# Gate rows of four gated layers: turned in pieces by VectorE, kept in DRAM and broadcast back, in place of matmuls against the identity

## The chip, the cores and the metric

The kernel runs on one NeuronCore of a Trainium2 chip. The metric is the device time of one execution in microseconds (us), taken as the median of the runs.

## The reference

The program is a chain of two networks over x of 256 rows and 1024 columns, all in float32. The first has four gated layers (pool, neighbourhood attention, convolution, pool), the second has two blocks, each a feed-forward part, a mixer and a second feed-forward part. What the change concerns is the gate of the first network:

```python
for i in range(DEPTH):                       # DEPTH = 4
    shift, scale, gate = _modulation(c, ada_w[i], ada_b[i])      # silu(c) @ w + b, cut in three
    hx = _rmsnorm(x, norm_g[i]) * (1.0 + scale[:, None]) + shift[:, None]
    ...                                      # yx = the layer's mixer of hx
    x = x + gate[:, None] * yx
    if update_ctx:                           # layer 0 alone
        ctx = ctx + cgate * yc
```

So a gate is one vector of 1024 values for each layer (and a second one, for the context rows, in layer 0). It multiplies the columns of the mixer's output, the same for every row.

## The kernel before

**Tiles and weights.** Rows lie on the 128 partitions: tiles t = 0, 1 are x, tiles t = 2, 3 are the context rows, which layers 0 and 1 also project. Each weight matrix comes in groups of 128x1024 float32 (512 KB) through eight slots `raw`. SyncE (SP) sends group g once group g-8 is used up (`send`); ScalarE (ACT) makes `w_hi` from it (`split`, L552), GpSimd (POOL) `w_lo` (`low`, L514), and TensorE (PE) multiplies three times with them (`mm3`, L1140 to L1142). So SP runs eight groups ahead of PE.

**Stages.** The list `PLAN` gives the order: p0_in (16 groups), p0_grp (2), p0_out (8), na_in (32), na_out (8), cv_in (32), cv_out (8), p3_in (16), p3_grp (2), p3_out (8), then the two blocks of the second network. Each engine's program is written out by hand in that order, and the engines meet through semaphores and counts.

**Modulation.** The 24 pieces of the modulation (6 for each layer) are computed beside the projections: `ada_weights(a)` on SP brings 2 MB into four places, two of which are `pt[:, 0:1024]` and `pt[:, 1024:2048]` and one `bias[:, 2048:3072]`; `ada_products` on PE; `ada_block` on VectorE (DVE, L1886 and L1888) puts the result as columns into `mods` (one value on each partition, eight columns each for shift, scale and gate of a layer). The last piece of layers 0 to 3 falls at group 7 of p0_in, group 7 of na_in, group 19 of na_in and group 11 of p3_in (`ADA_AT`).

**From columns to rows.** The sum needs the gate along the free dimension, the same on every partition. `gates` on PE (L1350) multiplies each column, broadcast, with the identity: eight products for a gate, in two PSUM banks, and `gate_rows` on ACT (L691) copies these into `pt`. `gated_sum` on DVE (L2008, L2011) multiplies a PSUM bank of the output projection with `pt` and adds the stream. There are five such calls:

- p0, x rows: between the two pairs of `turn_z(0, ...)`, which turn the product z of the grp stage. In front of the third `turn_z` stands a wait on `acc_free`, which DVE signals when it has made the second half of z (L2083).
- p0, context rows: between the third and the fourth output group of tiles 0 and 1.
- na: between the fourth output group and `last_chunks`, which adds groups 4 to 7 and needs each one's `w_lo`. After its `gate_rows`, ACT issues four loads of `rel_rows` (L557), loads a table (L574), splits three groups and takes the squares for the next layer's norm, on which PE's `turn_tile` waits (L1178).
- cv: behind the last projection block, ahead of the wait on `acc_free` for blocks 6 and 7, the second of which ACT gives after a Silu of two banks (L844).
- p3: as p0 with the x rows alone.

Of the kernel before, what the change touches and what calls it, by code (L numbers as in the profile page):

```python
# [5 lines left out]
F32 = mybir.dt.float32  # L6
# [5 lines left out]
P = 128  # L12
D = 1024
# [148 lines left out]
def program(nc, I, out, marks):  # L162
    na_rows = nc.dram_tensor("na_rows", (GRID_W, NA_ROW), F32, kind="Internal").ap()
    rel_rows = nc.dram_tensor("rel_rows", (LAYERS, P, REL_PITCH), F32, kind="Internal").ap()

    with ExitStack() as ctx:
# [25 lines left out]
        cond = sb("cond", [P, KC, 32])  # L192
        rope = sb("rope", [P, 2, NT, HD])
# [5 lines left out]
        eps = sb("eps", [P, 1])  # L199
        warm = sb("warm", [P, 16])  # L200

# [22 lines left out]
        decay_in = sem("decay_in")  # L224
        out_done = sem("out_done")
# [77 lines left out]
        def gate_bank(key, s, nb):  # L303
            return nb if key[0] == "p" and s == 0 else 4 + nb
# [41 lines left out]
        def _(sp):  # L346
# [31 lines left out]
            def narrow(w, blocks, nw, stage=None, prev=None, order=None):  # L378
# [9 lines left out]
                if stage:  # L388
                    for g in range(4 * blocks):
# [15 lines left out]
                        for a in ada_sent(stage, g):  # L405
                            ada_weights(a)
                    return
# [45 lines left out]

            def pool_weights(j, stage, prev=None):
                narrow(I["pool_w_in"][j], 4, 512, stage, prev)
                grp = I["pool_w_grp"][j].rearrange("g (c p) n -> p g c n", p=P)
                for h in range(2):
                    send(grp[:, 2 * h:2 * h + 2], [[512, 2], [256, 2], [1, 256]])
                wide(I["pool_w_out"][j], 8)

# [5 lines left out]
            for j in range(8):  # L466
# [4 lines left out]
                send(I["na_w_out"][0][j * P:(j + 1) * P, :], [[1, D]])  # L471
            narrow(I["conv_w_in"][0], 8, 512, "cv_in", "na_out", CV_ORDER)
            wide(I["conv_w_out"][0], 8)
            pool_weights(1, "p3_in", "cv_out")
# [66 lines left out]
        def _(act):  # L541
# [144 lines left out]
            def gate_rows(key, s=0):  # L686

                for nb in range(2):
                    act.wait_ge(pe_done, pe_s.count(("gate", key, s, nb)))
                    o = s * 1024 + nb * 512  # L690
                    act.activation(pt[:, o:o + 512], ps[:, gate_bank(key, s, nb), :], ACT.Copy).then_inc(act_done, act_s.one(("gate", key, s, nb)))  # L691

            def pool_layer(name, j, streams):
# [35 lines left out]
                gate_rows(name, 0)  # L729
                high_of_z(0, 2)  # L730
                high_of_z(0, 3)
                if streams > 1:
# [3 lines left out]
                    gate_rows(name, 1)  # L736
# [24 lines left out]
            def na_layer():  # L761
# [53 lines left out]
                gate_rows("na")  # L815

            def conv_layer():
# [28 lines left out]
                gate_rows("cv")  # L846
# [280 lines left out]
        def _(pe):  # L1127
# [222 lines left out]
            def gates(key, l, s=0):  # L1350

                for nb in range(2):
# [1408 lines left out]
```

## Time and profile before

| | |
|---|---|
| median of 3 runs | 1884.04 us (1882.99 to 1884.15) |
| the profiled execution | 1882.47 us, its span 1880.5 us |
| TensorE's mean granted clock | 0.998 |
| busy share of the span: PE, PE weight load, DVE, ACT, POOL | 99%, 82%, 41%, 49%, 72% |
| HBM over the span | 195 GB/s |
| SP's longest total wait | 1322.5 us, for PE to use up a weight group (L1142) |

The span is the time from the first to the last instruction. A busy share counts the time in which an instruction of the engine ran. In a timeline each line gives the start in us, the duration in us (of the whole group, where equal instructions are merged), the engine, the line of the code, the operation, what it writes and reads, and in brackets the idle time before it with what ended it. Matmuls overlap, so the time that one takes from PE is the distance between starts, not its duration. Of an instruction in float32 with 128 columns there are two records for one matmul of the code.

### The profile page before, as it was taken

To read this page: it belongs to the slowest core of one execution; us is meant where nothing else is said; L and a number is where in the kernel's file an instruction comes from. 1 tells how busy PE (TensorE), PEld (TensorE's weight loads), DVE (VectorE), ACT (ScalarE), POOL (GpSimd) and SP (SyncE) were. 2 spreads that over 40 slices of the span, in tenths; PEclk is the share of its full clock that TensorE was granted. 3 is DMA by queue.
4 is the path that set the end of the run, shared out by engine and by line. 5 is a ranking of instruction groups with operands and counts; after the bars stand their busy time and mean duration, and the time that the engine had idled before them with its cause. 6 is when DMAs were issued, how large, how long until landed. Compare 5 with 4: busy or idle time off the path is not lost.

```text
span 1880.5 us, 26918 instructions
## 1 busy us (share of the span) xinstructions
PE 1859.7 (99%) x10442; PEld 1534.1 (82%) x10442; DVE 779.9 (41%) x1421; ACT 916.6 (49%) x1365; POOL 1363.3 (72%) x568
## 2 busy tenths in 40 slices
PE   6999999999999999999999999999999999999999
PEld 5888788888888888888788888888888878888887
DVE  4213522674552440755630432533076563043253
ACT  3224511765455654555554454455355555446442
POOL 2524343456777698979678988879897957898886
PEclk9999999999999999999999999999999999999999
DMA  9762576439748476555455566656755644556663
GB/s 358 256 223 68 188 254 213 121 101 307 258 156 315 141 229 210 191 181 177 151 157 189 158 211 192 194 186 206 222 191 172 192 156 147 188 170 201 191 195 128
DMA packets 194846, 364.07 MB, mean 194 GB/s; under 512 B 32260, under 2 KB 48372, under 8 KB 194164
## 3 DMA queue, kind: packets, MB, share of 16 engines
q1 hardware_dynamic: 191280, 351.72, 58.6%
q10 hardware_dynamic: 3460, 10.88, 1.7%
q8 instruction: 74, 1.21, 0.3%
q14 instruction: 32, 0.26, 0.0%
HBM read 361.50 MB, written 6.10 MB: 195 GB/s over the span
## 4 chain that ended last, share of the span: by engine, by line
PE 96%; DMA 2%; ACT 1%; SPq 1%; DVE 1%; ACTq 0%; issue 0%
PE ps L1140 28%; PE ps L1142 27%; PE ps L1141 27%; PE ps L1158 2%; PE ps L1346 2%; DMA proj<-in_ada_w 1%; PE ps L1811 1%; PE ps L1809 1%; PE ps L1810 1%; PE ps L1725 1%; PE ps L1178 1%; PE ps L1498 1%; PE ps L1469 1%; PE ps L1479 1%; PE ps L1770 1%; SPq L375 1%
## 5 line engine op out<-in xcount | busy, mean ns | idle before, releaser
L514 POOL TENSOR_TENSOR w_lo<-raw,w_hi 128x1024 fp32r<-128x1024 f32 x556 | 1344.3, 2454 | 467.2 <-ACT w_hi L552 466.6
L552 ACT ACTIVATE w_hi<-raw 128x1024 fp32r<-128x1024 f32 x556 | 571.9, 1058 | 420.3 <-DMA raw<-in_ffn_w_up 99.8
L1140 PE MATMUL ps<-w_hi,xt_hi 128*128 128x512 f32 x1888 | 746.4, 395 | 3.3 <-POOL w_lo L514 2.5
L1142 PE MATMUL ps<-w_hi,xt_lo 128*128 128x512 f32 x1888 | 734.0, 389 | 0.0
L1141 PE MATMUL ps<-w_lo,xt_hi 128*128 128x512 f32 x1888 | 733.5, 389 | 0.0
L1140 PEld LDWEIGHTS ps<-w_hi,xt_hi 128*128 128x128 f32 x1888 | 355.3, 188 | 83.9 <-issue 11.2
L1142 PEld LDWEIGHTS ps<-w_hi,xt_lo 128*128 128x128 f32 x1888 | 355.0, 188 | 73.7
L1141 PEld LDWEIGHTS ps<-w_lo,xt_hi 128*128 128x128 f32 x1888 | 355.6, 188 | 68.1
L2307 DVE STREAM_TRANSPOSE ps<-proj 32x256 f32<-32x256 f32 (+1 forms) x384 | 166.6, 434 | 6.5
L1140 PE MATMUL ps<-w_hi,xt_hi_ctx 128*128 128x512 f32 (+1 forms) x432 | 167.6, 388 | 0.2
L1142 PE MATMUL ps<-w_hi,xt_lo_ctx 128*128 128x512 f32 (+1 forms) x432 | 166.7, 386 | 0.0
L1141 PE MATMUL ps<-w_lo,xt_hi_ctx 128*128 128x512 f32 (+1 forms) x432 | 166.7, 386 | 0.0
L2288 DVE TENSOR_TENSOR proj<-proj,ps 128x1024 f32<-128x1024 f32 (+1 forms) x18 | 20.4, 1132 | 252.2 <-PE ps L1142 247.8
L1140 PEld LDWEIGHTS ps<-w_hi,xt_hi_ctx 128*128 128x128 f32 x432 | 81.2, 188 | 17.1 <-DVE xt_lo_ctx L1964 1.0
L1142 PEld LDWEIGHTS ps<-w_hi,xt_lo_ctx 128*128 128x128 f32 x432 | 81.2, 188 | 16.3
L1141 PEld LDWEIGHTS ps<-w_lo,xt_hi_ctx 128*128 128x128 f32 x432 | 81.3, 188 | 15.8
L1886 DVE STREAM_TRANSPOSE qt<-ps 128x128 f32<-128x128 f32 x24 | 7.6, 316 | 148.8 <-PE ps L1158 148.8
L939 ACT ACTIVATE proj<-ps 128x1024 f32<-128x1024 f32 x20 | 20.6, 1028 | 63.9 <-PE ps L1142 63.9
L2021 DVE SCALAR_TENSOR_TENSOR x_res<-ps,x_res 128x512 f32<-128x512 f32 x24 | 16.6, 690 | 79.4 <-PE ps L1142 79.4
L868 ACT ACTIVATE proj<-ps 128x1024 f32 (+1 forms) x15 | 15.4, 1028 | 69.4 <-PE ps L1142 69.4
L2609 DVE TENSOR_TENSOR proj<-proj,ps 128x1024 f32<-128x1024 f32 x12 | 14.7, 1221 | 82.8 <-PE ps L1811 82.8
L521 POOL TENSOR_TENSOR bias<-bias,na_mask 128x1024 f32<-128x1024 f32 x8 | 19.1, 2394 | 32.7 <-DMA bias<-na_rows 32.7
(222 smaller groups left out, 1560.5 us busy)
## 6 DMA issues: line engine op xcount, KB each, us to landing
raw<-in_w_in SPq DMA_DIRECT2D x120, 512.0 KB, 3.6
raw<-in_ffn_w_gate SPq DMA_DIRECT2D x88, 512.0 KB, 4.4
raw<-in_ffn_w_up SPq DMA_DIRECT2D x88, 512.0 KB, 4.3
raw<-in_ffn_w_down SPq DMA_DIRECT2D x88, 512.0 KB, 4.2
pt<-in_ada_w SPq DMA_DIRECT2D x44, 512.0 KB, 5.2
raw<-in_pool_w_in SPq DMA_DIRECT2D x32, 512.0 KB, 8.5
raw<-in_na_w_in SPq DMA_DIRECT2D x32, 512.0 KB, 5.0
raw<-in_conv_w_in SPq DMA_DIRECT2D x32, 512.0 KB, 5.4
```

Of the source, the lines that this page charges most:

```text
L375: sp.dma_start(free(bias[64 * rq:64 * rq + 64, 0:1], [[64, 4], [1, GRID_W]], (hp % 2) * 1024 + h * 512 + t * 256), src).then_inc(bias_in[h ...
L514: pool.tensor_tensor(w_lo[:, s, :], raw[:, s, :], w_hi[:, s, :].bitcast(F32), ALU.subtract).then_inc(lo_done, 1)
L521: pool.tensor_tensor(both, both, free(na_mask[:, 0:1], [[0, 4], [1, SEQ]]), ALU.add).then_inc(bias_masked, 1)
L552: act.activation(w_hi[:, g % SLOTS, :], raw[:, g % SLOTS, :], ACT.Copy).then_inc(hi_done, 1)
L939: act.activation(pj(MIX_ORDER[n] * 512, 512, IN_COLS), pair_of(n), how).then_inc(acc_free[(b + n) % 2], 1)
L1140: pe.matmul(o, h, hi, start=start, stop=False)
L1141: pe.matmul(o, h, lo, start=False, stop=False)
L1142: return pe.matmul(o, c, hi, start=False, stop=stop)
L1158: last = pe.matmul(ps[32 * j:32 * j + 32, bank, 0:P], cond[:, m, :], free(ada_slot(k, a), [[P, 4], [1, 32]], c * 512 + 32 * j), start=m == ...
L1346: last = pe.transpose(ps[:, bank, c * SEQ + t * P:c * SEQ + (t + 1) * P], src(t, c), ident[:])
L2288: return dve.tensor_tensor(h, h, ps[:, at:at + 2, cols_of], ALU.mult)
L2307: last = dve.transpose(to, rows)
```

## The change

`gates` on PE and `gate_rows` on ACT are taken out, all five calls. In their place, for each layer l:

- **DVE** turns 32 columns of `mods` (the scale and gate columns of the layer) in 32x32 blocks into `gate_cols`, one instruction behind the layer's last modulation piece (`gates_turned`), after a wait that this piece has been written; from layer 2 on also a wait that the store of two layers before has ended.
- **SP** stores them with four DMAs, one for each 32 partitions, 16 rows of 128 bytes each (`keep_gates`), to `gate_scratch` in DRAM. It waits for DVE's turning first. It stands: for layer 0 behind the 16 sends of p0_in; for layer 1 in na_in behind the send of group 23; for layer 2 ahead of cv_in; for layer 3 behind the 16 sends of p3_in and ahead of those of p3_grp.
- **SP** brings each gate back with one DMA that reads 4 KB, in pieces of 512 bytes, for every one of 128 partitions (512 KB written; `gate_rows` of SP). It stands behind the eight output weight sends of the layer, after waits for the store and for the modulation weights that used the place. The place is `pt`, for na `bias[:, 2048:3072]`.
- `gated_sum` waits for that DMA in place of ACT's copy.
- `mods` is zeroed at the start, and `eps` moves into the last column of `warm`.

```diff
     na_rows = nc.dram_tensor("na_rows", (GRID_W, NA_ROW), F32, kind="Internal").ap()
+    gate_scratch = nc.dram_tensor("gate_scratch", (DEPTH, KC, 2, P), F32, kind="Internal").ap()
     rel_rows = nc.dram_tensor("rel_rows", (LAYERS, P, REL_PITCH), F32, kind="Internal").ap()
...
         cond = sb("cond", [P, KC, 32])
+        gate_cols = sb("gate_cols", [P, 2, 32])
         rope = sb("rope", [P, 2, NT, HD])
...
         rstat = sb("rstat", [P, 64])
-        eps = sb("eps", [P, 1])
         warm = sb("warm", [P, 16])
+        eps = warm[:, 15:16]
...
         decay_in = sem("decay_in")
+        gate_kept, gate_in = sem("gate_kept"), [sem("gate_in0"), sem("gate_in1")]
         out_done = sem("out_done")
...
-        def gate_bank(key, s, nb):
-            return nb if key[0] == "p" and s == 0 else 4 + nb
+        def gates_kept(l):
+
+            return 16 * 4 * (l + 1)
...
                             ada_weights(a)
+                        if stage == "na_in" and g == 23:
+                            keep_gates(1)
                     return
...
+            def keep_gates(l):
+
+                sp.wait_ge(dve_done, dve_s.count(("gate_cols", l)))
+                for j in range(4):
+                    sp.dma_start(bass.AP(gate_scratch.tensor, 2 * D * l + 32 * j, [[P, 2 * KC], [1, 32]]),
+                                 gate_cols[32 * j + 16:32 * j + 32, l % 2, :]).then_inc(gate_kept, 16)
+
+            def gate_rows(l, slots, free_at):
+
+                sp.wait_ge(gate_kept, gates_kept(l))
+                sp.wait_ge(ada_used, free_at)
+                for s, (where, o) in enumerate(slots):
+                    sp.dma_start(free(where[:, 0:1], [[P, KC], [1, P]], o),
+                                 bass.AP(gate_scratch.tensor, 2 * D * l + P * s, [[0, P], [2 * P, KC], [1, P]])).then_inc(gate_in[s], 16)
+
             def pool_weights(j, stage, prev=None):
                 narrow(I["pool_w_in"][j], 4, 512, stage, prev)
+                keep_gates(3 * j)
                 grp = I["pool_w_grp"][j].rearrange("g (c p) n -> p g c n", p=P)
...
                 wide(I["pool_w_out"][j], 8)
+                gate_rows(3 * j, ((pt, 0), (pt, D))[:2 - j], 4 * max(ADA_AT[stage].values()) + 2)
...
                 send(I["na_w_out"][0][j * P:(j + 1) * P, :], [[1, D]])
+            gate_rows(1, ((bias, 2048),), 4 * max(ADA_AT["na_in"].values()) + 3)
+            keep_gates(2)
             narrow(I["conv_w_in"][0], 8, 512, "cv_in", "na_out", CV_ORDER)
             wide(I["conv_w_out"][0], 8)
+            gate_rows(2, ((pt, 0),), 4 * max(ADA_AT["cv_in"].values()) + 1)
             pool_weights(1, "p3_in", "cv_out")
...
                         "p (c n) -> p c n", c=2), ACT.Copy).then_inc(act_done, act_s.one(("xhi", key, s, k)))
-
-            def gate_rows(key, s=0):
-
-                for nb in range(2):
-                    act.wait_ge(pe_done, pe_s.count(("gate", key, s, nb)))
-                    o = s * 1024 + nb * 512
-                    act.activation(pt[:, o:o + 512], ps[:, gate_bank(key, s, nb), :], ACT.Copy).then_inc(act_done, act_s.one(("gate", key, s, nb)))
...
                 high_of_z(0, 1)
-                gate_rows(name, 0)
                 high_of_z(0, 2)
...
                         high_of_z(1, k)
-                    gate_rows(name, 1)
                     split(3)
...
                 split(1)
-                gate_rows("na")
...
                                        ACT.Silu).then_inc(acc_free[(b + n) % 2], 1)
-                gate_rows("cv")
                 split(1)
...
-            def gates(key, l, s=0):
-
-                for nb in range(2):
-                    bank = gate_bank(key, s, nb)
-                    read_out(bank)
-                    for c in range(4):
-                        col = mods[:, 24 * l + 16 + nb * 4 + c, s:s + 1]
-                        last = pe.matmul(ps[:, bank, c * P:(c + 1) * P], free(col, [[0, P]]), ident[:],
-                                         start=True, stop=True)
-                    last.then_inc(pe_done, pe_s.one(("gate", key, s, nb)))
-                    held[bank] = (act_s, ("gate", key, s, nb))
-
             def pool_layer(name, l, streams):
...
                 turn_z(0, 1)
-                gates(name, l)
                 pe.wait_ge(acc_free[(b + 1) % 2], reads(b + 1))
...
                             turn_z(1, 2 * k + 1)
-                        if k == 2:
-                            gates(name, l, 1)
                 if streams > 1:
...
                 out_group(3)
-                gates("na", 1)
                 last_chunks("na_out", "naz", 4, 8, (0, 1), lambda k: k, "cv")
...
                     block(n)
-                gates("cv", 2)
                 go, bo = G0["cv_out"], B0["cv_out"]
...
             dve.memset(cond[:], 0.0)
+            dve.memset(mods[:], 0.0)
             dve.memset(stat[:], 0.0).then_inc(acc_free[1], 1)
...
+            def gates_turned(l):
+
+                dve.wait_ge(ada_read, ADA_COLS * (l + 1))
+                if l > 1:
+                    dve.wait_ge(gate_kept, gates_kept(l - 2))
+                dve.transpose(gate_cols[:, l % 2, :], free(mods[:, 0:1, 0:1], [[1, 32]], 2 * (24 * l + 8))).then_inc(dve_done, dve_s.one(("gate_cols", l)))
+
             def ada_beside(stage, n):
...
                     ada_block(a, bank_of(B0[stage] + n - 1, 3))
+                    if a % ADA_COLS == ADA_COLS - 1:
+                        gates_turned(a // ADA_COLS)
...
                 if t in (0, 2) and nb == 0:
-                    dve.wait_ge(act_done, act_s.count(("gate", key, t // 2, 1)))
+                    dve.wait_ge(gate_in[t // 2], 16 * (("p0", "na", "cv", "p3").index(key) + 1))
                 v = ps[:, bank_of(B0[stage] + nb, t), :]
-                o = (t // 2) * 1024 + nb * 512
-                dve.tensor_tensor(v, v, pt[:, o:o + 512], ALU.mult).then_inc(dve_done, dve_s.one(("gated", stage, t, nb)))
+                rows, o = (bias, 2048) if key == "na" else (pt, (t // 2) * D)
+                dve.tensor_tensor(v, v, rows[:, o + nb * 512:o + (nb + 1) * 512], ALU.mult).then_inc(dve_done, dve_s.one(("gated", stage, t, nb)))
                 dve.wait_ge(dve_done, dve_s.count(("gated", stage, t, nb)))
```

## Rows read from the trace of the kernel before

**Rows 1.** The page's busy line, and busy time by stretch, 640 us to the end.
```profile
PE 1859.7 (99%) x10442; PEld 1534.1 (82%) x10442; DVE 779.9 (41%) x1421; ACT 916.6 (49%) x1365; POOL 1363.3 (72%) x568
...
640.00:1881.00 1241.00, 1237.37 (x5793) 1020.04 (x5791) 515.92 (x973) 633.37 (x919) 1028.14 (x424) 1.00 0.59 183
```

**Rows 2.** The line of the gate products (L1357) and ACT's copies: count, durations.
```profile
L1357 PE MATMUL ps<-ident,mods x80: 270/276/276, 154.0 to 626.2; 128*128 128x128 f32 x80
...
L691 ACT ACTIVATE pt<-ps x10: 592/597/614, 155.2 to 626.5; 128x512 f32<-128x512 f32 x10
```

**Rows 3.** Timeline of DVE and PE, first gate block of p0.
```profile
153.35 2.36 DVE L2083 TENSOR_TENSOR proj<-ps,proj 128x1024 f32<-128x1024 f32 x2 [3.40 <-PE ps L1142]
...
154.02 1.95 PE L1357 MATMUL ps<-ident,mods 128*128 128x128 f32 x16
155.81 1.04 PE L1346 MATMUL ps<-ident,proj 128*128 128x128 f32 x8
```

**Rows 4.** Timeline of PE, second gate block of p0.
```profile
166.77 1.94 PE L1357 MATMUL ps<-ident,mods 128*128 128x128 f32 x16
168.47 0.48 PE L1140 MATMUL ps<-w_hi,xt_hi 128*128 128x512 f32 x1
```

**Rows 5.** Timeline of PE, POOL and ACT's queue, gate block of na and behind.
```profile
425.53 2.35 POOL L514 TENSOR_TENSOR w_lo<-raw,w_hi 128x1024 fp32r<-128x1024 f32 x1 [2.48 <-ACT w_hi L552]
...
425.56 1.95 PE L1357 MATMUL ps<-ident,mods 128*128 128x128 f32 x16
...
427.56 2.50 ACTq L557 DMA_DIRECT2D rel_rows<-in_rel  x4
...
429.43 0.39 PE L1140 MATMUL ps<-w_hi,xt_hi 128*128 128x512 f32 x1
...
437.42 1.09 PE L1178 MATMUL ps<-ident,proj 128*128 128x128 f32 x8 [0.35 <-ACT proj L602]
```

**Rows 6.** Timeline of PE, ACT and DVE, gate block of cv, first gated sum.
```profile
539.40 1.95 PE L1357 MATMUL ps<-ident,mods 128*128 128x128 f32 x16
...
539.60 1.02 ACT L844 ACTIVATE proj<-ps 128x1024 f32<-128x1024 f32 x1 [1.85 <-PE ps L1142]
...
541.11 0.48 PE L1140 MATMUL ps<-w_hi,xt_hi_ctx 128*128 128x512 f32 x1
...
556.01 0.70 DVE L2008 TENSOR_TENSOR ps<-ps,pt 128x512 f32<-128x512 f32 x1 [5.97 <-issue]
```

**Rows 7.** Timeline of DVE and PE, gate block of p3.
```profile
623.86 1.22 DVE L2083 TENSOR_TENSOR proj<-ps,proj 128x1024 f32<-128x1024 f32 x1 [1.65 <-PE ps L1142]
...
624.53 1.95 PE L1357 MATMUL ps<-ident,mods 128*128 128x128 f32 x16
...
626.32 1.04 PE L1346 MATMUL ps<-ident,proj 128*128 128x128 f32 x8
```

**Rows 8.** Timelines in p3: SP's send, DVE's last modulation piece, ACT's splits, ACT's Silu.
```profile
593.25 0.37 SPq L356 DMA_DIRECT2D raw<-in_pool_w_grp  x1
...
600.95 0.61 DVE L1888 TENSOR_TENSOR mods<-qt,cols 128x4 f32<-128x4 f32 x1
...
604.44 3.89 ACT L552 ACTIVATE w_hi<-raw 128x1024 fp32r<-128x1024 f32 x4
...
614.40 1.02 ACT L710 ACTIVATE proj<-ps 128x1024 f32<-128x1024 f32 x1 [6.07 <-PE ps L1142]
```

**Rows 9.** DMA: landing of two p3_grp sends, two small issues, a 4 KB row broadcast.
```profile
DMA to landing us min/median/max: 5.7/6.3/7.0
...
652.85 1.24 SPq L430 DMA_DIRECT2D mix_cols<-in_b_k_norm  x2
...
qt<-in_final_g ACTq DMA_DIRECT2D x1, 512.0 KB, 10.0
```

**Rows 10.** PE busy by stretch: start:end, length, busy (count), granted clock, DMA.
```profile
14.10:16.40 2.30, 1.17 (x36) 1.00 1.03 386
...
17.80:22.00 4.20, 3.72 (x40) 0.59 1.02 371
```

## The prediction, made before the changed kernel ran

> **What bounds the kernel now.** I read the page's busy line first: TensorE is busy for 99% of the span, the next engine for 72% [rows 1]. The chain that ended last runs almost wholly through PE. So time is won only where PE's own queue gets shorter, and lost only where PE begins to wait. From 640 us on PE is busy 1237.4 of 1241.0 us [rows 1] and the change touches nothing there, so what is won ahead of 640 us should reach the end whole. The second view is the line of the gate products: 80 records, which is 5 blocks of 16 [rows 2]. The third are the timelines around each block, where I look for the thing that would hold PE next if the block were gone. That is the whole question here.
>
> **What a block costs.** Between two groups of transposes the 16 records take 155.81 - 154.02 = 1.79 us of PE [rows 3], and the same in p3, 626.32 - 624.53 [rows 7]. Between matmuls with split weights it is 168.47 - 166.77 = 1.70 us [rows 4], and the first matmul behind the block starts its successor a little late, so I take 1.79 for all. Five blocks are 8.95 us, the most that the removal can give. ACT's ten copies of 0.6 us [rows 2] leave too. ACT is half idle, so they count only where ACT stands in front of PE.
>
> **Block by block.** A wait answered by another engine costs PE about 0.06 us; I add that to each release.
> - p0, x rows. The next transposes wait for DVE's second half of z, which ends at 153.35 + 2.36 = 155.71 [rows 3]. PE may go on at 155.77; it went on at 155.81. Won: 0.04. The block filled a wait that now opens, 1.7 us long.
> - p0, context rows. The next group's weights were split long before, and nothing else is asked for. Won: 1.79.
> - na. `last_chunks` asks for the low part of output group 7, which POOL ends at 425.53 + 2.35 = 427.88, so PE may go on at 427.94. PE reached that matmul at 429.43; without the block it gets there at 427.64 and waits 0.30 [rows 5]. Left: 1.49. But behind the block ACT's copies held four DMA issues (427.56), the table load, the splits and the squares on which PE's turning for the next layer waited 0.35 us at 437.42 [rows 5]. Without the copies ACT starts these issues some 3 us earlier, and PE only 1.5 us earlier, so that 0.35 goes as well. What is late next there is DVE's sum, which moves with PE. Won: 1.84.
> - cv. The output groups wait for the Silu that ends at 539.60 + 1.02 = 540.62, so PE goes on at 540.68 in place of 541.11 [rows 6]. Won: 0.43, with a new wait of 1.3 us.
> - p3. DVE's z ends at 623.86 + 1.22 = 625.08, so PE goes on at 625.14 in place of 626.32 [rows 7]. Won: 1.18, with a new wait of 0.6 us. ACT, then POOL, reach the splits behind their two copies earlier by about as much, so the next weights keep their distance.
>
> Sum: 0.04 + 1.79 + 1.84 + 0.43 + 1.18 = 5.3 us.
>
> **What is added, and what hides it.**
> - DVE: one turning for each layer. A turning of four times the columns is among the small instructions before L1888, which itself takes 0.61 us at most here [rows 8]; I put it at 0.3 with its wait, bounds 0.1 to 0.6. Four of them stand behind the last modulation piece, whose release to PE is given before. DVE is busy 41% [rows 1]. Cost: none. The zeroing of `mods` runs while DVE waits for parameters. The new wait of DVE on a store two layers back was answered long before.
> - SP: sixteen stores and five broadcasts in its queue. Two tiny DMAs took 1.24 us to issue [rows 9], so four stores take 2.5 us. Behind them wait the weight sends. For layers 0, 1 and 2 the columns are ready long before SP comes to them, and 2.5 us is small beside a lead of eight groups of 2.7 or 5.4 us each. Cost: none; the bound above is what the p3 case below gives.
> - Layer 3 is different: SP has to **wait** for the columns, and the two p3_grp sends and the first p3_out sends are queued behind that wait. DVE's last piece ends at 601.56 [rows 8], the turning at 601.9, the stores at 604.4. The first p3_grp send, at 593.25 before [rows 8], goes 11 us later. It landed 5.7 to 7.0 us after its issue [rows 9], among other traffic; alone I expect 4 to 5 for it, and the fourth of the burst about 8.5 after the first issue, at 613. ACT splits all four ahead of its Silu, which started at 614.40 when PE had finished the block [rows 8]. So ACT is ready at 614.0 to 614.5; taking 5.7 and more for the landing and 3.89 for the four splits it would be 614.0 to 615.3. Behind a late Silu come ACT's high parts, DVE's low parts, and then PE's grp products, which have about 0.5 us of their own to spare. Cost: 0 to 0.5 us, up to 1.5 if the stores issue slowly; I take 0.
> - The broadcasts. The nearest row of the same shape, 4 KB repeated on 128 partitions, landed after 10.0 us amid heavy traffic [rows 9]. Tightest is cv: the send before it is released when PE ends the last projection block at 539.40, so the broadcast is issued by 540.6, and its first reader started at 556.01, 555.6 after the gain [rows 6]. That leaves 15 us against 10, and the copies that stood there are gone. The DMA bytes that are added are 2.6 MB over five places. Cost: none.
>
 Each store has over 10 us until its broadcast, so by the rule and by the rows the sum is the same.
>
> **The rivals.**
> 1. *The clock falls in the new waits.* PE was busy 1.17 of 2.30 us around 15 us, waited again, and then ran 4.2 us at 0.59 of the clock, the low level of 1.2 GHz most of the time [rows 10]. The new wait in p0 is 1.7 us and that in cv 1.3, both between dense work. For it: the size of the wait is near that early case. Against it: there two waits followed each other, here one stands alone. Price: 4.2 x 0.41 = 1.7 us a place; p0 alone leaves 3.6 us won, p0 and cv 1.9: 1880.4 to 1882.1. Chance 0.16. The Trainium skill (TensorE: Matmul & The Clock Gate, The HAM clock gate) says that the throttled state is the default and that activity lifts it, so it makes this rival possible; by it I would not choose between one place and none.
> 2. *Layer 3's weights come late.* SP's wait holds p3_grp for more than the slack above: stores that issue in 1.2 us each, or landings of 8 us, make the Silu 3 to 4 us late and PE about 3 us: 1881 to 1882. Chance 0.10.
> 3. *The change gives less than the blocks say*: releases come later than modelled and only p0's second block and half of na are won, 2.5 us, 1881.5. Chance 0.06.
> 4. *Slower than before: a broadcast that is slow because 1024 pieces of 512 bytes come from one 4 KB of DRAM.* Its place is the first gated sum of cv, then p3 with some 16 us of room. It decides from a landing of 15 us; slower than before it gets past 20 us, since 5.3 us are to be eaten; at 28 us it costs 13 in cv and 12 in p3, about 1904. Against it: the 10.0 us of the row above. Chance 0.05.
>
> **How the numbers follow.** The forecast has 0.63. The profiled execution took 1882.47 us and would take 1877.2; its span goes from 1880.5 to 1875.2. It lies 1.57 below the median of 1884.04, and I count the gain from the median: 1884.04 - 5.3 = 1878.7. The forecast's own range is 1877 to 1880.2, with the late Silu and the run-to-run spread of about 1 us. 0.2% of the time is 3.8 us, about what a measurement of this kernel can tell from no change, so faster means below 1880.3. That takes the forecast but for a small part (0.60) and the milder end of rival 1 (0.06): 0.66. Rivals 1 to 3 for the rest and the forecast's weak end make no change: 0.28. Slower: rival 4 and a supply fault larger than described, 0.06. The range of 8 in 10 reaches down to 1876.6, where p3 or na give some tenths more, and up to 1882.4 over rivals 1 to 3.
>
> **What would show it.** PE's wait in front of the third transposes of p0 of about 1.7 us, ended by DVE L2083 of before; about 0.3 us on POOL in na; 1.3 us on ACT's Silu in cv; 0.6 us in p3; no wait of 0.35 us at the turning behind na; granted clock 1.00 at each. SP waits at the layer 3 stores, and ACT's four splits of p3 end just before PE's last block. DVE's first gated sums wait for sums, not for DMA. The prediction is wrong if a clock below 1.00 stands behind p0's new wait, if PE waits ahead of p3_grp, or if a gated sum of cv waits for its rows.

## The result: the changed kernel is slower by a quarter of a per cent

The changed kernel takes 1888.92 us, median of 17 runs (1884.35 to 1890.88); the kernel before took 1884.20 in as many (1882.99 to 1887.45). The ratio is 1.0025, 95% interval 1.0018 to 1.0031. The prediction was 1878.7, faster, with a range up to 1882.4: the change went the other way. The profiled execution of after took 1890.88 us with a span of 1889.1, some 2 us above its median, as that of before lay 1.7 below its own; I come back to those 4 us.

First the page's busy line of after and its line of the matmul that waits, which answer [rows 1]. PE's busy time is 3.8 us less (1855.9 for 1859.7), and the span 8.6 us more.

```profile
PE 1855.9 (98%) x10362; PEld 1527.1 (81%) x10362; DVE 794.9 (42%) x1426; ACT 912.1 (48%) x1355; POOL 1364.2 (72%) x568
...
L1155 PE MATMUL ps<-w_hi,xt_hi 128*128 128x512 f32 x1888 | 747.3, 396 | 12.0 <-DVE xt_lo L1972 9.0
```

The view that finds the loss is the list of waits of PE from 400 to 640 us (who waited for whom: us in total, times, the longest). In before the three waits there were 0.4, 0.4 and 0.3 us. In after:

```profile
PE ps L1155 <- DVE xt_lo L1972: 4.4, 2, 4.2
PE ps L1155 <- DVE mods L1887: 2.3, 1, 2.3
PE ps L1173 <- DMA proj<-in_ada_w: 1.2, 2, 0.7
PE ps L1155 <- issue: 1.2, 1, 1.2
PE ps L1361 <- DVE proj L2091: 0.4, 1, 0.4
PE ps L1155 <- DVE proj L2121: 0.4, 1, 0.4
PE ps L1155 <- POOL w_lo L540: 0.2, 1, 0.2
```

Of the short ones, three were forecast: 1.2 in front of cv's output weights (`issue`), 0.4 in p3 (L2091) and 0.2 on POOL in na. The one on L2121 stands in before too, and the 1.2 on `in_ada_w` are two waits for modulation weights. The first two in the list were not forecast: `xt_lo` is the low part of the turned input of the conv stage, `mods` the modulation piece. To see what each place gave or took, I set the start of the same PE instruction in both traces side by side:

| PE instruction | before | after | after - before |
|---|---|---|---|
| modulation products of p0, 113 us | 113.34 | 115.43 | +2.09 |
| third transposes of p0 | 155.81 | 157.85 | +2.04 |
| turning of the next layer, behind p0's second block | 202.75 | 202.95 | +0.20 |
| last transposes ahead of na's block | 421.94 | 421.43 | -0.51 |
| first matmul behind na's block | 429.43 | 427.46 | -1.97 |
| first turning for cv_in | 437.42 | 435.15 | -2.27 |
| first matmul that reads the second chunk of xt_lo | 440.07 | 441.87 | +1.80 |
| second turning for cv_in | 444.29 | 448.40 | +4.11 |
| last modulation products of cv (a = 21) | 520.18 | 525.99 | +5.81 |
| first turning of p | 533.08 | 543.11 | +10.03 |
| first output matmul of cv | 541.11 | 550.77 | +9.66 |
| third transposes of p3 | 626.32 | 634.72 | +8.40 |
| end of the span | 1880.5 | 1889.1 | +8.6 |

All five forecast gains are in it. They are 0.05, 1.84, 1.46 and 0.30 (na), 0.37 and 1.2 us, 5.2 in all. Against them stand three losses. 2.1 us had gone by 113 us, nearly all of it across PE's first wait for the turned x, which was 4.48 us here and 2.46 in the profile of before; I take no account of it, since kernels of before's kind below had 3.7 and 4.2 there too. Then **6.4 us** went between the first turning for cv_in and the second, and **4.2 us** between the last modulation products of cv and the turning of p. Another 1.7 went between 448 and 489 us, 1.2 of it in two waits for modulation weights that before didn't have in that execution, and 0.7 came back between 203 and 227 us, 0.4 of it a wait of before for such weights. I count both as chance of the two executions. 6.4 and 4.2 less 5.2 is 5.4, and the medians differ by 4.7. Of the 17 executions of after two took only 1884.35 and 1885.50 us; the losses are there in most executions, not in all.

**The first loss.** PE, ACT and SP's queue of after around the turning:

```profile
423.40 0.50 ACTq L583 DMA_DIRECT2D rel_rows<-in_rel  x1
...
423.94 1.92 ACTq L583 DMA_DIRECT2D rel_rows<-in_rel  x3
...
425.25 0.37 SPq L360 DMA_DIRECT2D raw<-in_conv_w_in  x1
...
435.15 1.09 PE L1193 MATMUL ps<-ident,proj 128*128 128x128 f32 x8
...
439.24 1.06 ACT L578 ACTIVATE w_hi<-raw 128x1024 fp32r<-128x1024 f32 x1 [4.14 <-DMA raw<-in_conv_w_in]
...
441.29 0.76 DVE L1972 TENSOR_TENSOR xt_lo<-ps,xt_hi 128x256 fp32r<-128x256 f32 x2 [4.30 <-ACT xt_hi L654]
...
441.87 0.77 PE L1155 MATMUL ps<-w_hi,xt_hi 128*128 128x512 f32 x1 [4.23 <-DVE xt_lo L1972]
```

In before the four copies of `rel` into DRAM (3 MB in all) were issued at 427.56 [rows 5], behind the gate copies, and SP's fourth group of `in_conv_w_in` at 425.76, ahead of them; ACT split that group at 437.27 without a wait. In after the copies go out from 423.40 on, and SP's group at 425.25, behind them. ACT's queue is in order: the split of that group stands ahead of ACT's share of the turned x, so ACT waits 4.14 us for a transfer, DVE waits for ACT, and PE waits for DVE. The chain of work that ended last passes through this transfer for 14 us:

```profile
424.99 0.24 PE ps L1157
425.25 13.97 DMA raw<-in_conv_w_in
439.61 0.59 issue
440.20 0.76 ACT ps L641 x2
```

What the DMA engines did meanwhile (queue, packets, MB, share of the engines; q1 is SP's queue, q10 is ACT's). After, 425.2 to 431 us, then 431 to 439.2:

```profile
q10 hardware_dynamic: 167, 1.26, 80.8%
q1 hardware_dynamic: 1, 0.00, 0.1%
...
q10 hardware_dynamic: 364, 1.72, 58.2%
q1 hardware_dynamic: 392, 0.77, 32.7%
```

And before, 425.8 to 431 us, with KB and us from issue to landing:

```profile
rel_rows<-in_rel ACTq DMA_DIRECT2D x2, 1280.0 KB, 10.6
raw<-in_conv_w_in SPq DMA_DIRECT2D x1, 512.0 KB, 3.5
```

So the same send landed 3.5 us after its issue when it stood 1.8 us ahead of the copies, and 14.0 when it stood behind the first of them: for 5.6 us not one of its packets went, while ACT's queue had the engines, and from then on the two shared them. The Trainium skill (DMA: Bandwidth & Descriptors, Queues, rings and completion order) has each engine take turns between the queues it has work for, packet by packet. From 431 us on the rows agree, with 392 packets of one queue and 364 of the other, and ACT's are more than twice as large (1.72 MB against 0.77). The 5.6 us ahead of that are no such turns; what held SP's first packet there was not found.

The wait is not the whole price. Inside it, from 440.1 us on, PE's clock was at the lower of its two levels, 1.2 GHz, and it stayed there for the first 5.0 us of work behind it. Stretches with busy time and granted clock (columns: length, busy time and instructions of PE, weight load, DVE, ACT, POOL, then clock, DMA share, GB/s), after:

```profile
441.80:447.20 5.40, 5.33 (x13) 4.26 (x14) 3.19 (x8) 2.60 (x9) 0.93 (x1) 0.53 0.88 311
...
538.60:541.00 2.40, 2.33 (x6) 1.89 (x7) 1.15 (x2) 0.00 (x0) 2.40 (x2) 0.60 0.17 68
541.00:546.00 5.00, 5.00 (x24) 4.12 (x23) 2.18 (x4) 1.52 (x3) 2.27 (x1) 0.85 0.31 97
```

From the matmul at 440.07 to the next turning, before took 4.22 us, after 6.53 for the same instructions: 2.3 us of clock on top of 4.1 of wait, 6.4. That is the ledger's step from -2.27 to +4.11.

**The second loss** is in the conv stage. DVE there makes the taps of the convolution (one multiplication and addition of a shifted 128x256 tile each, four to a group), then the product `p_made(0)`, then the last modulation piece, on which PE waits. DVE and POOL of before, then DVE and POOL of after:

```profile
516.26 5.95 DVE L2232 SCALAR_TENSOR_TENSOR proj<-proj,cols 128x256 f32<-128x256 f32 x4
522.24 3.31 DVE L2241 TENSOR_TENSOR proj<-proj 128x1024 f32<-128x1024 f32 x1
...
525.82 2.01 DVE L1888 TENSOR_TENSOR mods<-qt,cols 128x4 f32<-128x4 f32 x1
...
516.90 15.64 POOL L514 TENSOR_TENSOR w_lo<-raw,w_hi 128x1024 fp32r<-128x1024 f32 x6 [5.87 <-ACT w_hi L552]
```

```profile
520.32 1.80 DVE L2240 SCALAR_TENSOR_TENSOR proj<-proj,cols 128x256 f32<-128x256 f32 x4
522.15 0.74 DVE L2238 TENSOR_SCALAR proj<-proj,cols 128x256 f32<-128x256 f32 x2
522.93 10.12 DVE L2240 SCALAR_TENSOR_TENSOR proj<-proj,cols 128x256 f32<-128x256 f32 x4
533.09 3.30 DVE L2249 TENSOR_TENSOR proj<-proj 128x1024 f32<-128x1024 f32 x1
...
536.65 1.97 DVE L1887 TENSOR_TENSOR mods<-qt,cols 128x4 f32<-128x4 f32 x1
...
522.71 12.60 POOL L540 TENSOR_TENSOR w_lo<-raw,w_hi 128x1024 fp32r<-128x1024 f32 x5 [5.53 <-ACT w_hi L578]
```

Four taps of one form take 1.80 us while POOL is idle (0.45 each, at 520.32) and 10.12 while POOL splits weights (2.5 each, the length of one of POOL's instructions). In before the last four began 0.64 us ahead of POOL's burst, two of them went through free, and the four took 5.95. In after they began 0.22 us behind its start and all four were held. The Trainium skill (SBUF — State Buffer, Who interferes with whom) states the cause: a DVE instruction with two SBUF inputs and a GpSimd instruction that reads SBUF exclude each other for a whole instruction, and the one that comes second fully blocks. The rows agree, with 0.45 against 2.5 us. The piece then ended at 538.62, 12.6 us behind the a = 21 products; in before 7.65. PE can bear about 10.3: it went on at 538.67 after 2.34 us of wait, so it had been ready at 536.33, 10.34 behind the products. The loss of 4.2 us is 2.34 of wait and 1.9 at the lower level.

### The profile page after: what moved, and what is told of

It is laid out like the page before. It is cut to its first block, busy times and chain, and to the rows that moved or that the text cites. A ratio compares the mean times of both kernels' runs of the same rounds, so it can differ in the third digit from the quotient of the medians.

```text
span 1889.1 us, 26778 instructions
## 1 busy us (share of the span) xinstructions
PE 1855.9 (98%) x10362; PEld 1527.1 (81%) x10362; DVE 794.9 (42%) x1426; ACT 912.1 (48%) x1355; POOL 1364.2 (72%) x568
## 3 DMA queue, kind: packets, MB, share of 16 engines
q8 instruction: 74, 1.21, 0.3%
## 4 chain that ended last, share of the span: by engine, by line
PE 94%; DMA 3%; DVE 1%; issue 1%; ACT 0%; SPq 0%; ACTq 0%
PE ps L1155 27%; PE ps L1156 27%; PE ps L1157 27%; PE ps L1173 2%; PE ps L1361 2%; DMA proj<-in_ada_w 2%; PE ps L1809 1%; PE ps L1807 1%; PE ps L1808 1%; PE ps L1193 1%; PE ps L1723 1%; PE ps L1498 1%; PE ps L1469 1%; DMA raw<-in_conv_w_in 1%; PE ps L1479 1%
```

## The experiments

The theory has two parts: the earlier issue of the copies alone makes the first loss; the second is DVE's lateness where it meets POOL, and goes if PE's piece no longer stands behind the product that follows the taps. The rivals: the stores, the broadcasts or the new waits are dear in themselves, or it is where the buffers lie.

**Before, with the four copies issued ahead of the gate copies of na, nothing else.**

```
@@ na stage of ACT's program
+                rel_loads()
                 gate_rows("na")
```

> The kernel before, with ScalarE's four loads of rel_rows issued ahead of its two gate copies in the attention layer, and nothing else changed: PE still makes the gate rows. They then start near 424 us in place of 427.6, ahead of SP's send of the fourth cv_in weight group at 425.8. Theory A (the time of the change goes to these 3 MB, which get in front of that group; PE then waits for its first parts and the clock falls): PE waits 3 to 5 us at the first projection block of cv, some 2 us more are lost at the low clock, and the total is 4 to 9 us above the kernel before. Theory B (the stores, the broadcasts or SP's waits of the change make the DMA late): no such wait, total within 1 us of before.

Measured: 1887.27 us (1885.30 to 1889.63, 11 runs), ratio 1.0016, 1.0007 to 1.0025: 3.5 us slower by the medians, a little less than the 4 to 9 that theory A asked for. ACT's queue and PE:

```profile
424.18 0.50 ACTq L557 DMA_DIRECT2D rel_rows<-in_rel  x1
...
440.21 1.06 ACT L552 ACTIVATE w_hi<-raw 128x1024 fp32r<-128x1024 f32 x1 [3.03 <-DMA raw<-in_conv_w_in]
...
442.84 0.77 PE L1143 MATMUL ps<-w_hi,xt_hi 128*128 128x512 f32 x1 [3.12 <-DVE xt_lo L1967]
```

The wait and the low clock behind it stand in the kernel before, without any part of the change but the time of four DMA issues. So the first loss is not the price of what the change adds; it comes of what the change frees. It is a little smaller here (3.1 us of wait).

**After, with ACT holding the copies until the last group of na's output weights is split.**

```
+            act.wait_ge(lo_done, end_of("na_out") + 1)
             for l in range(LAYERS):
                 load(rel_rows[l, :, 0:REL_ROW], ...
```

> The changed kernel, with ScalarE waiting for POOL's low part of the last na_out group before it issues the four loads of rel_rows, so that they start near 427.4 us, behind SP's fourth cv_in send (425.3), as in the kernel before. Theory A: the wait of 4.2 us on DVE's low parts in cv is gone and the clock stays at 1.00; but the turning for the next layer now waits about 2 us for ScalarE, so na gives nothing: 3.4 us won of the 5.3 forecast if DVE's late modulation piece in cv goes too, total near 1881; if DVE's lateness at 538 us is a thing of its own, 1884 to 1885. Theory B: total stays at 1888 to 1889.

Measured: 1885.92 (1884.10 to 1888.12, 11 runs), 1.0010, 1.0001 to 1.0019. The copies now go out at 426.19, the wait on xt_lo is 0.17 us, but ACT's queue is held as well, and PE waits 2.00 us at the turning instead (436.00, on ACT L628), with no low clock. To hold an in-order queue is not the same as to move the issue in it. The wait of 2.33 us for the modulation piece stayed. The time is 0.9 us above the 1884 to 1885 that was expected for this case.

**Before, with the zeroed `mods`, DVE's turnings and the sixteen stores.** PE's gate products, ACT's copies and all reads stay.

```
+            dve.memset(mods[:], 0.0)
...
+                    if a % ADA_COLS == ADA_COLS - 1:
+                        gates_turned(a // ADA_COLS)
...
+                keep_gates(3 * j)
```

> The kernel before with what the change adds up to the stores: mods zeroed, DVE's four turnings and SP's sixteen stores at the places of the change, with their waits; no broadcast, and the gate rows still made by PE and copied by ScalarE, so the stored rows are not used. Theory A: SP's wait in p3 makes the p3_grp weights later but PE does not wait; total within 1 us of before. Theory B: the stores cost the time; total 3 us or more above before.

Measured: 1884.86 (1883.47 to 1885.97, 11 runs), 1.0001, 0.9992 to 1.0010. The medians on this chip lie 1.1 us apart and the interval reaches up to 1.0010, 1.9 us; beyond that the stores cost nothing that can be measured. PE waited 0.22 us for the modulation piece in cv, the first sign that this place has little to spare.

**After, with the copies issued in p3 instead of na.**

```
@@ pool_layer of ACT's program, at block 3 of p3
+                    if n == 3 and streams == 1:
+                        rel_loads()
```

> The changed kernel, with the four loads of rel_rows moved from behind the attention layer into p3, behind ScalarE's last splits of the input projection, where ScalarE waits for PE and the DMA is at half load. Theory A: no wait of 4.2 us in cv, no 0.35 us at the turning, the clock stays up, and the gain that was forecast appears: 5.3 us below before, 1878 to 1880, if DVE's late modulation piece in cv goes as well; 1882 to 1883 if that is a thing of its own. Theory B: 1887 or more.

Measured: 1882.67 (1881.29 to 1883.70, 11 runs), 0.9993, 0.9984 to 1.0002; 6.3 us below the changed kernel (5.9 when each is set against the kernel before that ran beside it), and the ledger above said 6.4. The wait on xt_lo is 0.17, the wait for the modulation piece 2.34 us at 530.23 as in after. The first part of the theory holds in both directions: added to before the early copies cost 3.5, taken from after they give about 6.

**Before, with the new buffers alone.**

```
+    gate_scratch = nc.dram_tensor("gate_scratch", (DEPTH, KC, 2, P), F32, kind="Internal").ap()
+        gate_cols = sb("gate_cols", [P, 2, 32])
+        eps = warm[:, 15:16]
```

> The kernel before with the new buffers alone: the DRAM tensor and the SBUF tile of the change are allocated, eps lies in the last column of warm, and no instruction is added or removed. Theory L (the late start of DVE's last taps in cv comes with where the buffers lie): the fourth weight group of cv_in sent by SP behind the modulation load lands about 8 us after its issue, as in the changed kernel and its three relatives with stores, DVE's last four taps take some 10 us together instead of 6, and PE waits about 2.3 us for the modulation piece at some 533 us: 1886.5. Rival S (it comes from the stores and turnings themselves): the landing stays at 7.1 us, the taps at 6 us, no wait of PE there: 1884.2, the time before.

Measured: 1883.62 (1883.06 to 1889.39, 11 runs), 1.0000, 0.9991 to 1.0009, no wait of PE for the piece. So the layout is not the cause of the time. The start of the split on which I had hung it was 0.6 us later than in before all the same.

**After, with the copies in p3 and the modulation piece made ahead of `p_made(0)`.**

```
                 taps(3)
-                p_made(0)
                 ada_beside("cv_in", 6)
+                p_made(0)
```

> The changed kernel with two edits: ACT's copies of rel into rel_rows are issued in p3 instead of na, and in the conv stage DVE makes the last modulation piece ahead of the product p_made(0) instead of behind it. Theory (the two losses found are all that ate the forecast gain): the wait of 4.2 us on xt_lo is gone as in the kernel with the loads in p3, and the modulation piece comes 3.3 us earlier, so that the wait of 2.34 us at some 530 us goes, and with it the stretch at low clock (1.9 us): 1878.5, 5.3 to 5.7 us below before. Rival (DVE is simply behind; the wait moves on to the turning of p, which now asks for p_made): PE waits 1 to 2.3 us at the turning in front of the last block of cv_in instead, 1881 to 1882.5, the time of the kernel with the loads in p3 alone.

Measured: 1879.07 (1877.67 to 1880.69, 9 runs), ratio **0.9973**, 0.9963 to 0.9983. The forecast for the change alone was 1878.7. DVE of this kernel:

```profile
514.20 10.13 DVE L2244 SCALAR_TENSOR_TENSOR proj<-proj,cols 128x256 f32<-128x256 f32 x4
524.36 0.32 DVE L1889 STREAM_TRANSPOSE qt<-ps 128x128 f32<-128x128 f32 x1
524.71 1.89 DVE L1891 TENSOR_TENSOR mods<-qt,cols 128x4 f32<-128x4 f32 x1
526.53 1.21 DVE L2253 TENSOR_TENSOR proj<-proj 128x1024 f32<-128x1024 f32 x1
```

DVE is as late as in after (10.13 us for the four taps), but what PE asks for ends at 526.60, 9.3 us behind the a = 21 products and inside the 10.3. And `p_made` takes 1.21 us in place of 3.30, because POOL has gone by. PE waits for neither. This version beats both kernels.

**Before, with the same two edits.**

> The kernel before with the same two edits (copies of rel in p3, the modulation piece ahead of p_made(0)) and without the change. It tells what of the time of the kernel with all three belongs to the change. Theory (before lost nothing at either place): the copies no longer sit in na, where PE waited 0.35 us at the turning, and nothing waits for the piece, so 1883.8 to 1884.2, and the change on top of the two edits is worth 5.3 us. Rival (the two edits are a gain of their own): 1880 to 1882, and the change on top of them is worth only 2 to 3 us.

Measured: 1883.32 (1882.18 to 1885.56, 11 runs), 0.9994, 0.9985 to 1.0003. Without the change the two edits give 0.5 us, not more than the noise; with it, on the same chip, 1883.32 becomes 1879.07, 4.3 us less by the medians and 5.2 by the spans of the two profiles (1881.4 and 1876.2), where 5.3 was forecast. The gates as rows from DRAM are worth most of what was forecast, once nothing is put in their way.

**After, with the second edit alone.**

> The changed kernel with the second edit alone: in the conv stage DVE makes the last modulation piece ahead of p_made(0); the copies of rel stay in na. Theory (two losses that add): the wait of 4.2 us on xt_lo at 441 us stays with its low clock, the wait of 2.34 us at some 538 us goes with its low clock of 1.9 us: 1888.9 - 4.2 = 1884.7. Rival (the second loss follows from the first, through the later start of the stage, and what it costs is hidden elsewhere): no more than 2 us are won, 1887 or more.

Measured: 1885.61 (1883.65 to 1887.38, 11 runs), 1.0006, 0.9997 to 1.0015; 3.3 us below after (3.9 below its second measurement, further down), where 4.2 was expected. The wait for the piece is gone, that on xt_lo there (4.96 us at 442.16). The two losses add.

**Before, with the turnings alone, and before, with the stores alone** (the first without a store, but SP still waits for each turning; the second from a tile that is zeroed once, so the rows stored aren't the gates, and nothing reads them). By now the question was which of the two moves DVE over the edge.

> The kernel before with the zeroed mods and DVE's four turnings alone; no store, no broadcast, PE's gate products and ACT's copies stay. The six kernels with stores all had, in the conv stage, the fourth weight group behind the modulation load ready for ACT 35.7 us ahead of PE's last modulation products (a=21); the four without had 36.0 to 36.8. Theory (the stores do it, through the transfers): here as without, 36.0 to 36.8 us, and no wait of PE for the modulation piece at 533 us. Rival (the turnings do it): 35.7 us, and DVE's last four taps blocked one by one (10 us together). Time by either: 1884 to 1885.

> The kernel before with the sixteen stores alone, at their places in SP's queue, from a tile that is zeroed once; no turning, so SP never waits for a column of gates; no broadcast, PE's gate products and ACT's copies stay. Theory (the stores do it): the group in cv is ready 35.7 us ahead of PE's last modulation products, and DVE's last taps start 3.1 us ahead of them, with a wait of PE for the piece of 0.2 to 2.3 us. Rival (the turnings do it, or it is chance): 36.0 to 36.8 us and no wait. Time: 1884 to 1886.5.

Measured: 1884.06 (1882.73 to 1888.79, 10 runs) and 1884.16 (1882.81 to 1887.34, 10 runs), ratios 1.0000 and 1.0002. In the profiled execution of the turnings PE waited 2.39 us for the piece, at 533.71; in that of the stores it didn't. But that execution of the turnings took 1887.38 us, 3.3 above its own median: the wait is then likely absent in most of its executions. What the two traces do show is the edge itself. Turnings, DVE and POOL:

```profile
517.76 10.33 DVE L2255 SCALAR_TENSOR_TENSOR proj<-proj,cols 128x256 f32<-128x256 f32 x4
...
517.71 2.40 POOL L529 TENSOR_TENSOR w_lo<-raw,w_hi 128x1024 fp32r<-128x1024 f32 x1 [5.69 <-ACT w_hi L567]
```

and stores:

```profile
517.83 8.27 DVE L2252 SCALAR_TENSOR_TENSOR proj<-proj,cols 128x256 f32<-128x256 f32 x4
...
518.25 2.40 POOL L533 TENSOR_TENSOR w_lo<-raw,w_hi 128x1024 fp32r<-128x1024 f32 x1 [5.64 <-ACT w_hi L571]
```

The four taps begin 0.64, 0.42 us ahead of POOL or 0.05 and 0.22 behind it, and take 5.95, 8.27, 10.33 and 10.12 us: two, one, none and none of them get through before POOL. Seven tenths of a microsecond decide over 4.4. All fourteen traces together show that there are two conditions. POOL's burst began 3.28 us ahead of the a = 21 products in every one of them; what moves is DVE's start, and the pause of POOL between its first and second instruction, in which one more tap goes through free if it is long enough:

| kernel | last four taps start ahead of the products | pause of POOL | the four took |
|---|---|---|---|
| before | 3.92 | 0.05 | 5.95 |
| before, stores alone | 3.69 | 0.24 | 8.27 |
| before, two edits | 3.68 | 0.43 | 6.12 |
| before, buffers alone | 3.53 | 0.75 | 6.15 |
| before, turnings alone | 3.23 | 0.22 | 10.33 |
| before, turnings and stores | 3.08 | 0.35 | 7.98 |
| after | 3.06 | none | 10.12 |
| the other five of after's kind | 3.08 to 3.26 | none | 10.12 to 10.27 |

The two left (before with the copies early, and the kernel of the last experiment below) began 4.05 and 3.99 ahead, POOL paused 0.39, and the four took 3.8. Neither theory of the two expectations is settled by one trace each.

**After, once more.**

> The changed kernel once more. Both theories of its two losses say that they are of the schedule and not of one execution: the wait of 4.2 us on DVE's xt_lo at some 441 us and the wait of 2.3 us on the modulation piece at some 538 us stand in the trace again, and the time is 1888 to 1889.5. If they were chance, one of them is missing here and the time lies 3 to 4 us lower.

Measured: 1889.50 (1888.74 to 1890.48, 6 runs), 1.0031, 1.0018 to 1.0043. Its waits were 4.15 us on xt_lo at 441.64 and 2.31 us for the piece at 536.71; its span was 1887.1, and its a = 21 products stood at 524.06, 1.9 us ahead of the first profile's: it was 0.9 ahead at the start, lost 0.4 of that on the way, and won 0.7 in a shorter stretch at the lower clock behind the first wait and 0.8 at a modulation load. Both losses belong to the schedule.

**Before, with the second edit alone.**

> The kernel before with one edit: in the conv stage DVE makes the last modulation piece ahead of p_made(0). The kernel with the turnings alone showed the wait of 2.4 us for that piece in its profiled execution, at 1887.4 us, while its median was 1884.1; and of 21 executions of the kernel before beside it, 7 lay above 1885.3. Theory (the kernel before stands at the edge: in some executions DVE's last taps fall behind POOL and PE waits for the piece, and the change only makes that the rule): without that dependence the upper tail is gone, nearly all executions lie between 1882.2 and 1884.5, the median falls by 0.3 to 1.0 us to some 1883.4, and PE never waits for the piece. Rival (the upper tail has other causes, as transfers at the start): about one in four executions above 1885.3 as before, median 1883.8 to 1884.4.

(Of those 21 executions, six lay above 1885.3, not seven.) Measured: 1883.51 (1882.13 to 1884.97, 11 runs), 0.9999, 0.9989 to 1.0008. The highest time came down, as that of the kernel with both edits had: one of 22 executions of these two lies above 1885.3, against 20 of the 100 of the kernel before that ran beside the experiments. The median didn't fall. So it is likely, but not shown, that before itself goes over the edge in some executions; what else feeds its upper tail stays open.

## Why the prediction was wrong

- **The gains: right, to tenths.** p0's first block gave 0.05 (forecast 0.04, wait 1.58 where 1.7 was said), the second 1.84 (1.79), na 1.46 and 0.30 (1.49 and 0.35), cv 0.37 (0.43, wait 1.16), p3 1.19 (1.18, wait 0.45): 5.2 for 5.3.
- **The step that failed first is the last sentences of na**: "ACT starts these issues some 3 us earlier", "so that 0.35 goes as well. What is late next there is DVE's sum". The issues did start 3.65 us earlier, counted from PE, and the 0.35 did go. But I read the four issues as time of ACT's queue (2.50 us in [rows 5]) and never as 3 MB of transfer. The question to ask was what SP sends in the window that they now precede, and who waits for it. The row was there: SP's send at 425.76, between the old place and the new one. It cost 6.4 us (4.1 of wait, 2.3 of clock), more than all gains.
- **The second is the term for DVE**: "DVE is busy 41% ... Cost: none." The share is a mean over the span. In cv from 516 us on DVE runs without a gap up to PE's modulation piece and had 2.7 us to spare (the piece 7.65 us behind the products, 10.3 can be borne). I bounded the turning's own time (0.1 to 0.6 us; it took 0.211) and not what a delay of tenths does to a chain that alternates with POOL. It cost 4.2 us. Which part of the change makes DVE late there is not settled. In the seven profiles that have stores and turnings both, ACT began to split the weight group that SP sends right behind a modulation load (476.48 in before) 35.7 to 35.8 us ahead of the a = 21 products, in the seven others 36.0 to 36.8; Buffers, turnings or stores alone gave part of that shift at most, and why the group lands later wasn't found. DVE's last taps began 3.06 to 3.26 us ahead of the products in the seven and with the turnings alone, 3.53 to 4.05 in the other six. POOL's pause is the second half: it is gone in the six kernels without PE's gate products, where ACT began its next split 2.04 to 2.84 us ahead of the products, and it is there, 0.05 to 0.75 us, in the eight with them (1.18 to 1.86 ahead). That these shifts are what the change does to DVE is likely, not shown.
- **The clock** (rival 1) fell in neither of the places that I named: p0's 1.58 us and cv's 1.16 left it at 1.00 (in the best version too). It fell with the waits of 4.23 and 2.34 us, and cost 2.3 and 1.9. The price of 1.7 from [rows 10] was near, its places weren't, and the two unforeseen waits had it as an addition.
- **Layer 3's supply** (rival 2) and **a slow broadcast** (rival 4) didn't come. The stores and the broadcast in the page's list of transfers of after (KB each, median us to landing):

```profile
pt<-gate_scratch SPq DMA_DIRECT2D x4, 512.0 KB, 5.4
bias<-gate_scratch SPq DMA_DIRECT2D x1, 512.0 KB, 4.8
gate_scratch<-gate_cols SPq DMA_DIRECT2D x16, 2.0 KB, 4.8
```

  Four stores took SP 1.72 us at 611.51 (2.5 was said). The last of ACT's four splits ended at 622.36, the Silu behind began at 623.99. The broadcast bound of 10.0 us [rows 9] was twice too long.
- **The rivals as a set** were wrong in kind. Two of them asked what the added stores and broadcasts cost, one what the clock does in the opened waits, one whether the blocks give less; none asked what the removed parts had held back. "Slower" had 0.06, 0.05 of it on the broadcast and the rest on a supply fault. The later end of na's gate copies was a brake on a 3 MB transfer, and nothing in the code says so.

## What to carry to other kernels

When an edit lets a queue run ahead, list everything that the queue issues in the next microseconds, DMA bytes too, and look up which sends of other queues it now precedes and who waits for them. A mean busy share says nothing about an engine that stands in front of the bound engine for one stage; measure from its output there to the latest time at which it is wanted, and where DVE and POOL work on SBUF together count that distance in whole POOL instructions. When a change costs more than it should, look for the losses before dropping it: two moved pieces of code turned 1888.9 us into 1879.1.

## What the runs showed of the hardware

- A DVE instruction of 0.45 us with two SBUF inputs takes 2.5 us next to POOL's splits; a start 0.64 us ahead of POOL or 0.05 behind it made 5.95 or 10.33 us of the same four, and a pause of POOL of 0.35 us or more let one more through free (7.98 us with a start 0.20 behind). Those with one tensor input were held too: the two of L2238 at 499.14 in after took 4.30 us, 0.74 where POOL was idle. The turning of 32 columns took 211 or 212 ns in all four places.
- A send of 512 KB issued 1.8 us behind the first of four copies of 3 MB in all from another queue landed after 14.0 us, with its first packet 5.6 us after the issue; issued 1.8 us ahead of them it landed after 3.5.
- Waits of PE of 1.16, 1.58 and 2.00 us between dense work left the granted clock at 1.00; behind waits of 2.34 and 4.23 us PE did 3.4 and 5.0 us of its work at the low level. All other waits of 2.3 us and more behind 100 us, in six more profiles, were followed by it too.
